# A decoder step on one Trainium2 core: TensorE's loop over expert pairs made longer, the eight-slot ring started earlier

## What is computed

```
logits = rmsnorm(x) @ w_router + b_router;  top 4 of 32, softmax over the four
for each expert e:   z = xb @ w_up[e] + b_up[e]              (1024 x 2048)
                     y = min(z_even,7)*sigmoid(1.702*min(z_even,7))*(clip(z_odd,-7,7)+1)
                     out += weight * (y @ w_down[e] + b_down[e])   (1024 x 1024)
y_prompt, y_sample = rmsnorm(x + out) * norm_final
```

## Time and profile before

| | |
|---|---|
| median of 3 runs | 1134.74 us (1133.98 to 1135.69) |
| profiled execution | 1134.97 us, of which the span of the profile is 1133.2 us |
| TensorE matmul busy | 1103.4 us (97%) |
| TensorE weight load busy | 491.7 us (43%), beside the matmuls |
| VectorE busy | 313.6 us (28%) |
| ScalarE busy | 228.7 us (20%) |
| DMA | 437.99 MB, mean 387 GB/s over the span |
| matmuls of line 1407 (up) | 424.7 us |
| matmuls of line 1445 (down) | 220.6 us |

### The profile page before, as it was taken

One profiled execution on the slowest core, in us unless ns is written; L12 is line 12 of the kernel. 1 busy time (PEld: TensorE's weight loads), 2 busy tenths in 40 slices (PEclk: granted clock), 3 DMA queues, 4 the chain that ended last, 5 costly groups with the idle time before them and its releaser, 6 DMA issues.

```text
span 1133.2 us, 14624 instructions
## 1 busy us (share of the span) xinstructions
PE 1103.4 (97%) x5774; PEld 491.7 (43%) x5774; DVE 313.6 (28%) x794; ACT 228.7 (20%) x635; POOL 34.6 (3%) x71
## 2 busy tenths in 40 slices
PE   9999999999999999999999999999999999999997
PEld 6788878844243333333433333333332323233322
DVE  6565662122212121213221313030303021212123
ACT  3663454412020101010101010111110101010103
POOL 1200012200000000000000000000000000000000
PEclk9999999999999999999999999999999999999999
DMA  9743528999999999999999999999999999999995
GB/s 349 292 162 116 166 105 341 408 397 421 429 427 430 436 427 430 433 429 431 422 426 434 427 431 436 428 430 437 428 430 436 429 430 436 429 426 428 427 423 235
DMA packets 31263, 437.99 MB, mean 387 GB/s; under 512 B 5616, under 2 KB 7944, under 8 KB 10360
## 3 DMA queue, kind: packets, MB, share of 16 engines
q1 hardware_dynamic: 30592, 435.64, 91.7%
q10 hardware_dynamic: 624, 1.68, 0.4%
HBM read 436.00 MB, written 2.41 MB: 387 GB/s over the span
## 4 chain that ended last, share of the span: by engine, by line
PE 73%; DMA 22%; DVE 2%; issue 1%; ACT 1%; SPq 0%; DVEq 0%
PE bank L1407 26%; DMA ring<-in_experts 21%; PE bank L1445 16%; PE bank L1113 10%; PE bank L1159 5%; PE bank L1303 4%; PE bank L1282 3%; PE bank L1227 1%; PE bank L1316 1%; PE bank L1306 1%; DVE area L1861 1%; PE bank L1279 1%; PE bank L984 1%; PE bank L995 1%; DMA ring<-in_opening 1%
## 5 line engine op out<-in xcount | busy, mean ns | idle before, releaser
L1407 PE MATMUL bank<-ring,area 128*64 128x512 f32 x1872 | 424.7, 597 | 7.3 <-DMA ring<-in_experts 6.9
L1407 PEld LDWEIGHTS bank<-ring,area 128*64 128x64 f32 x1872 | 126.6, 136 | 276.2 <-issue 254.0
L1445 PE MATMUL bank<-ring,area 128*64 128x512 f32 x960 | 220.6, 599 | 5.9 <-DMA ring<-in_experts 5.8
L1849 DVE TENSOR_TENSOR x_tok<-x_tok,bank 128x512 f32<-128x512 f32 x60 | 41.3, 688 | 326.6 <-PE bank L1303 326.6
L862 ACT ACTIVATE area<-area 128x256 f32<-128x256 f32 x64 | 26.7, 417 | 513.7 <-DVE area L1861 513.7
L1113 PE MATMUL bank<-ring 128*128 128x264 f32 (+1 forms) x512 | 119.6, 391 | 0.0
L1445 PEld LDWEIGHTS bank<-ring,area 128*64 128x64 f32 x960 | 63.5, 136 | 122.8 <-issue 107.2
L1113 PEld LDWEIGHTS bank<-ring 128*128 128x128 f32 x512 | 95.8, 190 | 20.0 <-issue 1.3
L1886 DVE TENSOR_TENSOR area<-area 128x1024 f32<-128x1024 f32 x15 | 18.4, 1225 | 209.5 <-ACT area L872 209.5
L1303 PE MATMUL bank<-area 128*128 128x512 f32 x128 | 71.8, 644 | 0.0
L1159 PE MATMUL bank<-area,ring 128*128 128x264 f32 x256 | 58.6, 387 | 0.0
(11 more groups left out here) (292 smaller groups left out, 685.6 us busy)
## 6 DMA issues: line engine op xcount, KB each, us to landing
ring<-in_experts SPq DMA_DIRECT2D x64, 4096.0 KB, 24.9
ring<-in_experts SPq DMA_DIRECT2D x36, 2048.0 KB, 30.4
ring<-in_experts SPq DMA_DIRECT2D x24, 1024.0 KB, 9.0
ring<-in_w_in SPq DMA_DIRECT2D x16, 1024.0 KB, 9.5
area<-in_experts SPq DMA_DIRECT2D x7, 2048.0 KB, 13.1
area<-in_experts SPq DMA_DIRECT2D x3, 4096.0 KB, 20.8
ring<-in_w_out SPq DMA_DIRECT2D x8, 1024.0 KB, 4.8
area<-in_experts SPq DMA_DIRECT2D x4, 1024.0 KB, 8.3
```

The lines of the kernel that those rows point to most:

```text
L1407: m = mm(bank[2 * h + n][64 * e:64 * e + 64, :], xe[:, k, 64 * e:64 * e + 64], w[:, kk, e, NB * n:NB * (n + 1)], start=False, stop=(k == K ...
L1445: m = mm(bank[4 + c][64 * e:64 * e + 64, :], y_t[:, 4 * half + f, 64 * e:64 * e + 64], w[:, f, e, :], start=False, stop=(half == 1 and f = ...
L1849: eng.tensor_tensor(x, x, combined_bank(unit, last)[:, :], ALU.add).then_inc(s.added, 1)
```

## The change

`RINGED` goes from 71 to 59 and `RING_PLACES` is turned to `(8, 0, 4, 6)`, so that the ring of eight starts one pair (12 loads) earlier; twins 59 and 61 keep the waits of the ring of ten. `OPEN_PAIRS` goes from 6 to 5, and TensorE's loop has five turns, for pairs 5 to 14; the other engines' loops that start at `OPEN_PAIRS` start one pair earlier. The norm products go with `OPEN_PAIRS - 1`, from pair 5 to pair 4. The two places in `area` are then used last by loads 53 and 54, and VectorE gets a wait for `ring_used` of 55 (`LAST_EXTRA` is 54) ahead of `ones_rows`. SyncE's loop becomes one of four twins with 14 turns. Twins go up to load 178. Load 179 is single and signals on the odd place of its pair of slots; load 180 (`LONE`) signals on a semaphore of its own, left from the opening.

```diff
-TWIN, TWIN_END = 35, 169
-RINGED = 71
-RING_PLACES = (0, 4, 6, 8)
-OPEN_PAIRS, TURN_PAIRS = 6, 2
+TWIN, TWIN_END = 35, 179
+LONE = TWIN_END + 1
+RINGED = 59
+RING_PLACES = (8, 0, 4, 6)
+OPEN_PAIRS, TURN_PAIRS = 5, 2
...
-TURN_ROUNDS = (PAIRS - 2 - OPEN_PAIRS) // TURN_PAIRS
+TURN_ROUNDS = (PAIRS - 1 - OPEN_PAIRS) // TURN_PAIRS
...
+LAST_EXTRA = max(n for n in range(WIDE + 1, LOADS) if wide_place(n) in EXTRA)
...
-    return wide_place(n) | 1 if twin(n) else wide_place(n)
+    return wide_place(n) | 1 if twin(n) else wide_place(n) | (n == TWIN_END)
...
+    if n == LONE:
+        return 0
...
-            with eng.Fori(0, TURN_ROUNDS) as it:
-                for n in range(RINGED, RINGED + TURN_LOADS, 2):
-                    eng.wait_ge(s.ring_used, TURN_LOADS * it + (n + 1 - RING + 1))
-                    twin_dma(n, TURN_LOADS // 2 * it)
-            for n in range(RINGED + TURN_LOADS * TURN_ROUNDS, TWIN_END, 2):
+            for n in (RINGED, RINGED + 2):
+                eng.wait_ge(s.ring_used, n + 1 - WIDE + 1)
+                twin_dma(n, 0)
+            turns = (TWIN_END - RINGED - 4) // RING
+            with eng.Fori(0, turns) as it:
+                for n in range(RINGED + 4, RINGED + 4 + RING, 2):
+                    eng.wait_ge(s.ring_used, RING * it + (n + 1 - RING + 1))
+                    twin_dma(n, RING // 2 * it)
+            for n in range(RINGED + 4 + RING * turns, TWIN_END, 2):
                 eng.wait_ge(s.ring_used, n + 1 - RING + 1)
                 twin_dma(n, 0)
...
-            pair(PAIRS - 2, wide_full(PAIR_LOADS * (PAIRS - 2)), True)
             pair(PAIRS - 1, wide_full(PAIR_LOADS * (PAIRS - 1)), True, last=True)
...
             add(OPEN_PAIRS - 2)
+            eng.wait_ge(s.ring_used, LAST_EXTRA + 1)
             eng.memset(ones_rows, 1.0)
```

More of the change, by code:

```diff
@@ L537, in _ @@
                 i = n - (LOADS - PAIR_LOADS)
-                dst, full = place(wide_place(n))
+                dst, full = place(wide_place(n))[0], open_loaded[1] if n == LONE else place(signal_place(n))[1]
                 eng.wait_ge(s.ring_used, n - RING + 1)
@@ L1338, in full @@
                         return front
+                    if n == LONE:
+                        eng.wait_ge(open_loaded[1], 32)
+                        return place(wide_place(n))[0]
                     count = 16 * landed(signal_place(n), range(n + 1))
```

## The result

The changed kernel takes 1142.28 us in the median (1141.39 to 1143.15, 4 runs) against 1134.87: a ratio of 1.0062, 95% interval 1.0050 to 1.0075, slower by 7.4 us. The forecast was 1138.8 with a range up to 1141.4. The sign was right, the size was not: 7.4 in place of 3.9. The profiled execution took 1143.15 us, 8.2 more than that of before.

A forecast was written before the change was run, and what follows sets the result against it. The prediction took TensorE's pace to bound the kernel up to 783 us and the stream of expert loads after that. Its terms, +3.3 + 1.0 - 0.3 = +4.0 us, gave 1138.8 us, range 1136.6 to 1141.4.

The forecast's parts named there:

- part 1: Norm products and VectorE's new wait: PE stalls 4.35 us in pair 4 in place of 0.37, +3.98 us on PE.
- rival 3: TensorE's clock falls to 1.2 GHz in pair 4's stall, work takes 2.2 us longer, 1141.0 us in all; chance 8%.
- part 2: Ring of eight from load 59: twin 65, issued at 501.3 to a nearly empty queue, puts the stream 3.3 us late.
- The estimate of 11.6: Twin 65's flight from an empty queue by the skill page: 11.6 us, a gap of 2.5 us; 12.4 was taken.
- a hole opens only if the issue comes after the last landing: Expert load stream: a late issue delays later landings when the DMA queue runs empty; twin 65's hole put at +3.3 us.
- part 3: Twins up to 178: pair 15's first down load starts at 1106.74 against 1105.70, +1.0 us, the stream's saving included.
- part 4: Loops: some five fewer code transfers, -0.3 us; extra loop turns costed at nothing.
- Part 4's remark that the trace disagrees with the rule on taken branches: PE's loop: the rule adds a fetch per extra turn, but PE's waits hold no such entry; turns costed at nothing.
- That the stream would not be broken: Twin 65 is queued early enough, only the tail remains, 1135.5 us; decides if load 58 is done before about 499; chance 12%.
- rival 4: Faster: five code transfers vanish from the last engine, 3.0 us go, and 0.4 by the twins, 1131.3 us; chance 4%.

The follow-up runs named there:

- experiment 6: Also spelled `stall_filled_18`: changed kernel with eighteen wide bf16 matmuls of ones in TensorE's pair 4 stall; 1140.14 us, ratio 1.0043.
- stall_alone: Kernel before with one wait more, VectorE waiting for load 66 ahead of ones_rows in pair 5; ring, loops and twins as before; 1138.23 us, ratio 1.0025.
- stall_filled: Changed kernel with ten wide bf16 matmuls of ones into a free bank during TensorE's pair 4 stall; 1142.11 us, ratio 1.0060.
- experiment 8: Kernel before with loads 169 to 178 sent two at a time and nothing else; 1136.66 us, ratio 1.0014.
- experiment 2: Changed kernel with VectorE's wait, ones_rows and diag moved behind the first half of pair 4's gating; 1137.6 us, ratio 1.0020.
- wait_53: Changed kernel with VectorE waiting for load 53 (54 loads) instead of 55 loads; 1137.62 us, ratio 1.0022.

## Why the prediction was right in sign and too small

**The bound and the stall (part 1)** were right. PE stalls 4.41 us (4.35 forecast), and what follows goes by way of late issues to the stream: filling the stall, shifting the norm operations and shortening the norm matmuls each move twin 65 and the time together.

**The clock** is the first step that failed: the sum has no term for it. I had it as rival 3 with 8%, at 2.2 us. It happened, in all four runs of the changed kernel (mean granted clock 0.996 or 0.997, against 0.999 in the trace of before), and made TensorE 3.0 us later at load 58: 504.3 against the 501.3 of part 2, all other terms being as forecast. I had argued from the earlier trace rows, where TensorE is idle for 4.9 us at a clock of 1.00. That misread the rows. The second of them has the clock at 0.50 with TensorE still idle, so the clock fell in that gap too, only later in it. Here it was still 1.00 up to 480.0, 3.7 us into the stall, and 0.50 from 480.1 on. The Trainium skill, "TensorE: Matmul & The Clock Gate", section "HAM oscillation", says that waits for data between groups of matmuls, when they are long enough, make the array throttle again. It was the better guide, and the trace agrees with it here. The price in the time is about 2.1 us by experiment 6, and 2.9 us at the landing of twin 65 (515.2 for 518.1).

**The hole in the stream (part 2)** had the right place and a term too small: twin 65 took 13.5 us where the sum has 12.4. Twin 63, from an empty queue, took 12.2 us, so that the 12.4 I had worked out was right for that. The estimate of 11.6 by the Trainium skill, "DMA: Bandwidth & Descriptors", section "Anatomy of one DMA", is below it; that section has its figures from transfers that GpSimd issues, and these are issued by SyncE. What made twin 65 take 1.1 us more isn't shown by a run, but the traces point at one thing. It was issued 0.9 us before the twin ahead landed, and so was twin 63 of experiment 6, which took 12.4. Twin 75 of `stall_alone`, issued 1.5 us before, took 12.3. The difference is in the queue of code (q8): in the changed kernel a transfer of code of 16 KB starts at 513.8, in the flight of twin 65, and one lies in the flight of every such twin that took 13.0 us or more (65 in `stall_filled` and `stall_filled_18`, 77 in `stall_alone`); in the flights of the two that took 12.3 and 12.4 there is none.

By the same rows, "a hole opens only if the issue comes after the last landing" is wrong. Without a transfer of code in the way, twins that were issued 3.2 to 4.0 us before the landing ahead came 9.7 us after it in three cases and 10.0 to 11.2 us after it in four; with a lead of 4.9 us or more all but one kept 9.7. The 24 us to landing of the earlier trace rows lie on the safe side and could not show the edge. The norm matmuls had therefore a price of their own, even without a stall; I had let them only add to it.

**The tail (part 3)**: its length was exact, 1063.03 to 1113.88 is 50.85 us, forecast 50.86. Its price was put at 1.0 us and measured, in experiment 8, at 1.5, with 1.0 inside the interval.

**The loops (part 4)** were mis-sized too, on the other side. The page counts 30 transfers of code in place of 34. The stream came 7.9 us late at twin 67 (514.4 + 13.7, against 520.2 for before, issued at 495.2 with 25.0 to landing), but 7.15 at load 177 (1063.03 against the 1055.88 of part 3): 0.7 us came back, where part 4 had 0.3. The trace of before shows where. Its twin 89 landed 11.0 us after twin 87 (617.6), and a transfer of code fell in between:
```profile
L484 SPq DMA_DIRECT2D ring<-in_experts x1: 333/333/333, 608.8 to 608.8; - x1
...
DMA to landing us min/median/max: 19.8/19.8/19.8
```
```profile
q8 instruction: 1, 0.02, 0.6%
```
The second view is that of the window 617.6 to 628.6. In the changed kernel no code is moved from 615 to 1090 us, and the twins there come 9.7 us apart throughout. Taken over all ten traces, 586 twins issued between 430 and 1035 us were issued more than 5 us before the landing ahead of theirs. In 505 cases no transfer of code began between the two landings or in the microsecond before, and one of these twins came more than 9.85 us after the one ahead. In 81 cases one did, and 23 of these twins came that late, the worst of them about 1.5 us behind the pace. So a transfer of code often costs nothing and sometimes over 1 us. No run took the transfers away by themselves; the link is one of place and time. Part 4's remark that the trace disagrees with the rule on taken branches goes too far: in before no code is moved from 659 to 1017 us, so the turns of the loop fetched nothing, and the rule, which is on branches to code that must be fetched, was not put to the test.

**The sum by its terms** for the profiled execution: 3.3 forecast for the hole, 3.0 of clock (504.3 for 501.3) and 1.6 for issues and flights longer than I had them make the 7.9 of twin 67. Less the 0.7 that came back, and with 1.0 of tail, that is 8.2.

**The rivals.** Rival 3, the clock, was the one that came, and its 1141.0 is still 1.3 us short: it priced the clock at 2.2 in place of 3.0 and kept the flight of 12.4. That the stream would not be broken (12%) needed load 58 before about 499; it was done at 504.3, and by experiment 2 even 497.4 is too late. What rival 4 (4%) built on, transfers of code that hold the stream up, shows in the traces, but at about 1 us and not at 3.

## What to carry to other kernels

When transfers run at the full rate, a delay of the computing engine is free only while the next transfer is issued well before the one ahead of it lands. Compare that lead with the shortest one at which the pace holds, not with zero: for the 4 MB transfers here a lead of about 5 us held wherever no transfer of code fell in (but for one twin in 505), and one of 3 to 4 us did so only at times. Before moving a small step ahead of a semaphore wait, ask what the waiting engine has queued behind it: here a wait for load 54 with two operations of 1.2 us, put ahead of the gating, cost 5 us, and behind its first half nothing. A gap in TensorE's work as long as this one (4.4 us) should be priced with the clock, and a row of another gap should be read to its end before it is called harmless. When a stream of loads is the bound, look for the transfers of code in it as well.

## What the runs showed of the hardware

In the changed kernel and in `stall_alone` the granted clock fell to 0.50 within an idle stretch of 4.41 us, 0.6 and 1.1 us before its end, and stayed there for 6.8 us. In `stall_filled` TensorE did 2.1 us of work on constant operands and was then idle for 2.04 us; the clock fell when it was at work again and was 0.50 for 3.4 us, in the window 482.0 to 485.3. It did not fall after 1.58 us of idleness (`wait_53`, and the earlier trace rows), nor in `stall_filled_18`, with 0.29 us. A transfer of 4 MB took 12.2 us from an empty queue and 12.3 to 12.4 us when issued 0.9 to 1.5 us before the one ahead landed, against 13.0 to 13.6 us with a transfer of code of 16 KB in its flight, though the bytes alone pass in 9.7.
